# Moving the log-forget subtraction ahead of the three rotary rotations on VectorE

## The reference, cut to what matters

```
proj = einsum('btd,de->bte', h, w_in)
fq, fk, fv, ff, rq, rk, rv, rg = split(proj, ...)
logf = log_sigmoid(ff + b_f)                     # forgetting attention: 8 numbers per token
rq = rotary(rq.reshape(B, T, 4, 64), pos)        # retention: 4 heads of 64
rk = rotary(rk.reshape(B, T, 4, 64), pos) * 64 ** -0.5
```

## Time and profile before

| | |
|---|---|
| median of 3 runs | 1088.59 us (1086.52 to 1092.72) |
| the profiled execution, own time | 1086.52 us |
| its span in the profile | 1084.7 us |
| PE busy | 998.3 us, 92% of the span |
| DVE busy | 414.7 us, 38% |
| ACT busy | 262.7 us, 24% |
| POOL busy | 14.2 us, 1% |
| mean granted clock of TensorE | 0.964 |

### The profile page before, as it was taken

One profiled execution on the slowest core, in us unless ns is written; L12 is line 12 of the kernel. 1 busy time (PEld: TensorE's weight loads), 2 busy tenths in 40 slices (PEclk: granted clock), 3 DMA queues, 4 the chain that ended last, 5 costly groups with the idle time before them and its releaser, 6 DMA issues.

```text
span 1084.7 us, 14905 instructions
## 1 busy us (share of the span) xinstructions
PE 998.3 (92%) x5814; PEld 621.9 (57%) x5814; DVE 414.7 (38%) x828; ACT 262.7 (24%) x576; POOL 14.2 (1%) x24
## 2 busy tenths in 40 slices
PE   6999998997799999999979999779689999999996
PEld 4888877786555445454435555358654454454543
DVE  0514524434413332233322888841523133323332
ACT  3413324224122112211222222341212221122110
POOL 0101000000000000000000000000000000000000
PEclk9999999998899999999999999789799999999998
DMA  9514532029199899888930227300439988988841
GB/s 383 230 48 148 149 127 79 1 79 404 51 423 376 338 381 368 352 340 340 407 127 1 79 79 311 103 1 2 153 138 423 369 345 337 397 353 353 340 196 58
DMA packets 34825, 249.09 MB, mean 230 GB/s; under 512 B 4016, under 2 KB 4168, under 8 KB 5784
## 3 DMA queue, kind: packets, MB, share of 16 engines
q1 hardware_dynamic: 33120, 238.66, 55.1%
q0 software_dynamic: 1664, 9.86, 2.9%
HBM read 243.47 MB, written 5.44 MB: 229 GB/s over the span
## 4 chain that ended last, share of the span: by engine, by line
PE 77%; DVE 6%; ACT 2%; issue 1%; ACTq 0%; DVEq 0%
PE PS L851 21%; PE PS L875 11%; PE PS L922 9%; PE PS L842 9%; PE PS L972 8%; PE PS L741 6%; PE PS L488 3%; PE PS L718 2%; PE PS L989 2%; PE PS L798 1%; PE PS L894 1%; DVE X L1626 1%; PE PS L861 1%; DVE YC L1716 1%; DVE YD L1716 1%
## 5 line engine op out<-in xcount | busy, mean ns | idle before, releaser
L851 PE MATMUL PS<-slot,XG 128*64 128x512 f32 x1024 | 226.1, 594 | 3.6 <-ACT XG L1202 3.6
L851 PEld LDWEIGHTS PS<-slot,XG 128*64 128x64 f32 x1024 | 72.2, 137 | 142.3 <-issue 140.4
L488 PE MATMUL PS<-slot,HT 128*128 128x256 f32 x576 | 134.2, 390 | 10.8 <-DMA slot<-in_w_in 10.8
L488 PEld LDWEIGHTS PS<-slot,HT 128*128 128x128 f32 x576 | 110.5, 195 | 28.0 <-DMA slot<-in_w_in 10.8
L875 PE MATMUL PS<-slot,HID 128*64 128x512 f32 x512 | 120.3, 613 | 6.1 <-issue 4.8
L1619 DVE SCALAR_TENSOR_TENSOR YL<-PS,GATE,YH 128x1024 fp32r<-128x1024 f32 x32 | 41.1, 1284 | 190.6 <-ACT YH L1222 190.6
L1626 DVE TENSOR_TENSOR X<-X,PS 128x512 f32<-128x512 f32 x96 | 66.0, 687 | 104.0 <-PE PS L922 104.0
L842 PE MATMUL PS<-G,XHI 128*128 128x256 f32 x384 | 98.0, 294 | 4.9 <-ACT XG L1202 3.4
L842 PE MATMUL PS<-G,XLO 128*128 128x256 f32 x384 | 94.8, 286 | 0.0
L922 PE MATMUL PS<-YH,GT 128*128 128x512 f32 x192 | 82.2, 428 | 5.7 <-DVE YL L1619 5.7
L972 PE MATMUL PS<-HC,slot 128*128 128x384 f32 x256 | 86.0, 491 | 1.6 <-DVE HC L1676 1.6
(11 more groups left out here) (286 smaller groups left out, 977.0 us busy)
## 6 DMA issues: line engine op xcount, KB each, us to landing
slot<-in_experts SPq DMA_DIRECT2D x192, 1024.0 KB, 8.7
slot<-in_w_in SPq DMA_DIRECT2D x12, 1024.0 KB, 12.0
slot<-in_w_pw SPq DMA_DIRECT2D x12, 1024.0 KB, 7.4
slot<-in_w_out SPq DMA_DIRECT2D x4, 1024.0 KB, 5.0
KTC<-in_k_past POOLq DMA_DIRECT2D x1, 2048.0 KB, 13.5
slot<-in_v_past SPq DMA_DIRECT2D x2, 1024.0 KB, 8.2
HT<-in_x_feat SPq DMA_DIRECT2D x2, 768.0 KB, 5.8
X<-in_x_tok SPq DMA_DIRECT2D x1, 1536.0 KB, 12.3
```

The costliest lines, as they stand in the source:

```text
L488: last = mm(PS[:, 6 + n % 2, 0:UCOL], HT[:, k, P * t:P * (t + 1)], w[:, k, :], start=k == 0, stop=k == KD - 1)
L851: last = mm(PS[CAP * e:CAP * (e + 1), 2 + pair, :], XG[:, k, CAP * (2 * pair + e):CAP * (2 * pair + e + 1)], w[:, 2 * FE * (k % 4):2 * FE ...
```

## The change

The wait for `ff_ln` and the subtraction are taken from behind the three rotations and put ahead of them, directly behind the three small instructions on `FF`. No instruction is added or dropped, and the other engines' programs are the same word for word.

```diff
             q.link(V.scalar_tensor_tensor(lt, ff, -1.0, ff, ALU.mult, ALU.max), S("ff_abs"))
             ts(FF[:, :, :], FF[:, :, :], 0.0, None, ALU.min)
+            dve.wait_ge(S("ff_ln"), 1)
+            tt(LF[:, :, :], FF[:, :, :], LT[:, :, :], ALU.subtract, S("lf_ready"))
 
             x1 = PJ[:, :, RQO:RVO].rearrange("p t (g h d) -> p t g h d", h=2, d=RK // 2)
...
             for t in range(NT):
                 dve.wait_ge(S("pj_ready"), NT + t + 1)
                 rotate(t)
-            dve.wait_ge(S("ff_ln"), 1)
-            tt(LF[:, :, :], FF[:, :, :], LT[:, :, :], ALU.subtract, S("lf_ready"))
             dve.wait_ge(S("ret_in"), 16)
```

## The result

The changed kernel took 1102.3 us (median of 6 runs, 1100.95 to 1103.32) against 1092.3 us for the kernel before (6 runs, 1086.52 to 1092.99): the ratio is 1.0105, 95% interval 1.0086 to 1.0126. It is slower, as forecast, and by about the amount: 10.0 us by these medians where 9.8 were worked out. But the time of 1098.4 us is 3.9 too low, and 1102.3 lies just above the range. The three new runs of the kernel before took 1092.3 to 1093.0 us, so the level from which the forecast started, 1088.6, was itself 3.7 us too low.

A forecast was written before the change was run, and what follows sets the result against it. TensorE, busy 998.3 of 1084.7 us, was taken to bound the kernel. A 7.1 us hole at its first transposes plus 2.7 us of low clock gave 9.8 us on 1088.6, so 1098.4 us, range 1093 to 1102.

The forecast's parts named there:

- second hole: Further TensorE wait at the later transposes or scores; forecast to cost 0, everything in time by over a microsecond.
- the distance: Delay of the scores at 53.35, some 9 to 10 us, forecast to be the same at the start of the experts.
- The clock term: TensorE at half clock behind the hole at its first transposes; 2.7 us taken.
- the ends 1.6 and 3.5: Bounds in us of the half-clock loss, from TensorE's restarts at 139.79 and 187.16.
- the lower end of the sum, 7.0: Lower bound in us of the total loss forecast as 9.8; the upper was 10.8.
- the third measure: Kernel start as gauge of the clock loss: three pieces took 13.54 us against 10.63 later, 2.9 us more.
- the router's 1.71 us: Full-clock time of one matmul group at the router, against 3.60; a clock fall there was said to cost 1.9 us.
- the highest of three runs is no likely median: Reason for cutting the range's top from 1103.5 to 1102 us.
- The third rival: Not slower: low clocks after 139.79 and 187.16 go away, 5.1 us come back, time 1093.3; chance 0.08.
- The second rival: A second hole or longer low clock costs another 3 us, about 1101.5; chance 0.06.

The follow-up runs named there:

- e2: Changed kernel with 16 extra matmuls, result unused, ahead of TensorE's first transposes; 1098.2 us, ratio 1.0093 to the kernel before.
- e3: Changed kernel with the wait and subtraction put between the first and second rotation; 1096.1 us, ratio 1.0050 to the kernel before.
- e4: Changed kernel with the wait and subtraction put between the second and third rotation; 1092.1 us, ratio 0.9998 to the kernel before.
- e6: Kernel before with only the wait for ff_ln moved ahead of the rotations, the subtraction left behind them; 1101.2 us, ratio 1.0106.
- e7: Changed kernel with ScalarE computing LT ahead of the evacuation of pieces 4 and 5; 1091.5 us, ratio 1.0010 to the kernel before.
- e5: Changed kernel run again without edit, beside new runs of the kernel before; 1101.7 us, ratio 1.0113.
- e1: Changed kernel with projection pieces 6 and 7 ahead of TensorE's first transposes; 1093.1 us, ratio 1.0027 to the kernel before.
- e12: Changed kernel with 16 extra matmuls behind piece 6, after the hole; 1109.3 us, ratio 1.0168 to the kernel before.
- e10: Changed kernel with 8 extra matmuls at the start of TensorE's hole; 1102.3 us, ratio 1.0093 to the kernel before.

## Why the prediction came out as it did

**The mechanism was right.** The rows named for the stretch around the change appeared: VectorE idle for 9.46 us (9.4 forecast), LF and the stores unmoved, a wait of 6.9 us for VectorE at the transposes (7.1), no second hole, transfers without effect, the low clock behind the restart. e2, e3, e4, e6 and e7 each alter one link of that chain, and the loss changes as the link has it. One sign needs a profile of the same sort to be read. The forecast had the distance "unchanged at the start of the experts", and against the profile of before it grew from 9.4 to 14.2 us. But that profile was of the high group. e4 is no different from the kernel before to L529 and was profiled in the low group, as the changed kernel was. The experts' first matmuls in e4, and then in the changed kernel:

```profile
276.66 0.74 PE L826 MATMUL PS<-SE,cst 128*128 128x96 f32 x2 [5.86 <-DVE SE L1303]
```

```profile
286.43 0.74 PE L826 MATMUL PS<-SE,cst 128*128 128x96 f32 x2 [5.86 <-DVE SE L1303]
```

From L504 (29.21 and 28.84) that is 247.45 and 257.59: 10.1 us, and 8.5 us for e5 by the same count. Among profiles of one sort the distance holds within 1 us.

**The clock term, local part: 2.3 us** in the first profile and 1.7 in the profiles of e5 and e6 (8.79 and 8.52 less later transposes by 7.06 and 6.83), inside the ends 1.6 and 3.5 and under the 2.7 taken. Three details of its working were off without deciding anything: the lower end of the sum, 7.0, left the clock out altogether (7.0 + 1.6 would be 8.6); the third measure, the slow first pieces, shows in the pace alone, since the granted clock of the rows is 1.00 all through them; and the router's 1.71 us are the chain's count, where the timeline has 1.87 for the same matmuls, so that they lose 1.7 and not 1.9.

**The step that failed is the level from which the sum was made.** "On their median of 1088.6 the forecast is 1098.4": the median of three runs was taken as the kernel's level. With 68 executions the kernel before has two levels, 25 executions at 1083.5 to 1089.2 us with a mean clock of 0.962 or more (median 1087.5), and 43 at 1091.5 to 1093.9 us at 0.960 or less (median 1092.7). Two of the three known runs came from the first sort. The profiled executions of before and e4 show one of each: two programs that differ by the place of the wait and the subtraction behind the second or the third rotation, the same to L529 within 0.01 us, and then 0.93 against 0.80 as the mean clock between 180 and 230 us. No slower execution of the kernel before itself was profiled, but over all kernels the two go together: 0.93 in the five profiles of the high group (before, e1, e2, e7, e12), 0.80 to 0.83 in the nine of the low one. e4's windows there:

```profile
180.00:230.00 50.00, 45.41 (x385) 36.84 (x383) 20.21 (x44) 16.86 (x39) 0.00 (x0) 0.80 0.06 22
```

The span of the three runs, 6 us, showed that something differed between executions; it went into the range only as a spread, and "the highest of three runs is no likely median" cut off just the part where the result fell. The highest of the three, 1092.7, is the median of the more frequent group. That the difference of the medians, 10.0 us, came so near to the 9.8 worked out is in part luck: the six executions of the kernel before had four of the slower sort, and the figure moves between 9.5 and 11.7 with the mixture.

**The clock term, far part, was left out.** The changed kernel's 17 executions are all of the slower sort (median 1102.2). Against the same sort of the kernel before they are 1102.2 - 1092.7 = 9.5 us longer, which is the hole and the clock behind it. Over all executions the means differ by 1102.3 - 1090.6 = 11.7 us; the other 2 are the 25 of 68 executions, 5.2 us faster each, that no longer occur: 25/68 x 5.2 = 1.9. The third rival had the sign wrong: it let later low stretches go away, and they became the rule. The second rival, with a chance of 0.06, was nearer, in that later falls of the clock came out worse; but it had them as a further 3 us on every execution, and against the same sort there is none of it. That a preceding hole does this, and a busy shift of the same length does not (2 of 40 against 10 of 18 in the high group), is shown by counts; how it does is open. e10 to e12 changed the length of the idle time and the shift behind it, and the group stayed rare.

**The profiled pair misleads.** Its spans differ by 15.7 us, more than any of the averages, since the profile before was of the faster sort and the one after of the slower.

## What to carry to other kernels

An instruction that waits holds back all that stands behind it on its engine; before moving one forward, take the slack of the next thing that the bounding engine needs from the trace, here 2.6 us against a delay of 9.6. On an engine that is busy without a break, a hole cost here its length and then the low clock behind it, even from 2.6 us of idle time, and filling half of it did not help. Before a change of 1% is worked out against a base, sort the executions of the base by their granted clock: a median of three can be a mixture of two levels, here 5.2 us apart.

## What the runs showed of the hardware

The mean granted clock of an execution explains most of the spread of one program: the kernel before ran from 1083.48 us at 0.967 to 1093.89 at 0.957, and 0.010 x 1090 us = 10.9 is the difference of 10.4. The 14 profiles, of programs that differ little, had low stretches of about 7 us or of 17 to 20 us at the same place (0.93, and 0.83 to 0.80, over 50 us), although TensorE was busy for 44.5 to 45.4 of these 50 us either way. Behind a hole of 2.57 us (e3) as well as behind one of 3.44 (e10) and 6.89 the clock was low; behind 1.77 us (e1) it stayed high.
